# A hybrid decoder step: its first normalized input made one feature chunk at a time, with GpSimd scaling the sample tokens there

## The chip, the cores and the metric

The kernel runs on one core of one Trainium2 chip. A core has TensorE (PE, matrix products into PSUM), VectorE (DVE), ScalarE (ACT), GpSimd (POOL) and SyncE (SP, here used only to issue DMAs). The engines run their own instruction streams in order and meet by semaphores. The metric is the device time of one execution in microseconds, lower is better.

## The reference, cut to what matters

The model is a decoder trunk with two layers (`DEPTH = 2`), width 1024, run on 256 prompt tokens and 64 sample tokens (8 sequences of 8). Every layer is a SwiGLU of half weight, a token mixer and another such SwiGLU, and each of these sub-layers is normalized and modulated by vectors made from the conditioning `c` of its sequence:

```python
def modulate(h, shift, scale):
    return h * (1 + scale) + shift
...
    silu_c = jax.nn.silu(c)
...
        mod = (silu_c @ p['w_ada'][l] + p['b_ada'][l]).reshape(B, N_MOD, D)
        m = [mod[:, j][:, None, :] for j in range(N_MOD)]
        hh = modulate(rmsnorm(x, p['g_pre'][l, 0]), m[0], m[1])
```

There are nine modulation vectors of 1024 features for each layer. The first SwiGLU needs vector 0 (shift) and vector 1 (scale) of layer 0, which are a product of `silu(c)` (9 conditions: one prompt, eight samples) with 2048 columns of `w_ada`, 8 MB of weights. Later, the recurrent mixer of layer 1 needs `softplus(-rg_lambda)`, a function of 1024 parameters alone.

## The kernel before

Tokens are columns: 320 of them (256 prompt, 64 sample). Features are cut into `KC = 8` chunks of 128 partitions. Every product is made in three passes (`three_passes`, L1663 to L1667): a value is kept as a high and a low part, and high x high, low x high and high x low are summed in PSUM. So a weight tile that arrives in `w_raw` is split by ACT (`w_hi`, L1948) and DVE (`w_lo`, L2142), in two halves of 128x1024, and the normalized input by ACT (`xn_hi`, L2006) and DVE (`xn_lo`, L2218). A weight tile of the SwiGLU (`gu`) holds a gate block and an up block; its products are 2 blocks x 8 chunks x 3 passes = 48 matmuls of 128x320. The product of one tile with one chunk (6 matmuls) is called a unit below; unit (y, k) is tile y with chunk k.

The front is what comes before the first SwiGLU (`gate0`). SP issues the loads in a fixed order: `cT`, then pieces of `w_ada` (`a_raw`, 512 KB, six slots), `x`, small tables, further pieces, and the first half tiles of `gu` late. The plan is the table `ADA_PLAN`: a piece p holds contraction chunk p % 8 of vector p // 8. Each piece is four matmuls (`ada_pieces`, L1737) in four column groups of PE. A vector is complete only after its eight pieces. Then ACT copies it out (`ada_row`, L1962), PE turns it to feature rows with `sel4` (`ada_transpose`, L1756), and DVE adds the bias (`ada_bias`, L2153) and makes scale factors (`scale_factors`, L2162). Vector 0 takes pieces 0 to 7, vector 1 pieces 8 to 15. Small products of `ident` with `x` (`fill`, L1745) stand between pieces; their result is not used.

Beside that, ACT squares `x` (L1993), DVE sums the squares (L2417), PE sums over partitions (L1764), ACT and DVE make one over the root, PE spreads it (`spread`, L1772), and DVE scales `x` into `f` (`scale_x`, L2427). Once the vectors are there, ACT modulates the prompt columns of a chunk (`modulate`, L2001), DVE the sample columns of all chunks in a few instructions (L2228), ACT makes `xn_hi`, DVE `xn_lo`, and PE starts the units of the first two tiles (`two_tiles`, L1685), where tile 1 runs two chunks behind tile 0, so that units (1,5), (1,6) and (1,7) stand behind (0,7).

In the other stages GpSimd modulates the sample columns of chunks 2 to 7 (`samples`, L561 and L563). GpSimd also issues the `w_ada` pieces of the later stages (`ada_load`, L570).

After the first two tiles, `gate_up` runs 20 tiles more. Its start is a chain: when unit (0,7) is done, ACT splits the first half of tile 2 (L1948) and makes `sil` (L2026), DVE makes `w_lo` and `hbuf` (L2309), and PE may start tile 2 when `hbuf` is there. `gate1`, the second SwiGLU, starts in the same way behind `normed("gate1")` on DVE.

`softplus` is a row of small DVE instructions on 128x8, nearly all waiting for the one before. Its two first steps (L2433, L2435) and ACT's exponential (L2102) run in the front, the other 18 (L2441 to L2461, one of them eight times) inside the input projection of the attention stage (`dve_even`, at block 17).

## Time and profile before

| | |
|---|---|
| median of 3 runs | 1385.54 us |
| the runs | 1385.26 to 1385.80 us |
| span of the profiled execution | 1384.7 us |
| PE busy | 1340.4 us (97%) |
| DVE busy | 784.0 us (57%) |
| ACT busy | 621.2 us (45%) |
| GpSimd busy | 111.1 us (8%) |
| DMA, mean over the span | 188 GB/s |
| DMA, first of the 40 slices | 360 GB/s |

The profile is of one execution, whose span from first to last instruction is 1384.7 us; the device time of the runs is 0.8 us more than that. Records of PE overlap, since matmuls are pipelined: a matmul of 128x320 has a record of 0.31 us while the next one starts earlier. So the spacing of starts tells how fast PE works, not the length of a record. An fp32 matmul (the pieces, `fill`, `spread`) shows as two records.

### The profile page before, as it was taken

Reading aid. Unit: us, or ns where it says so; the run is one execution under the profiler, and the core shown is the slowest. Engines: PE = TensorE matmul, PEld = TensorE weight load, DVE = VectorE, ACT = ScalarE, POOL = GpSimd, SP = SyncE. Lnnn points to the kernel's source line nnn. Section 1 sums busy time; section 2 is a strip of 40 time slices with the busy share of each in tenths; the row PEclk is TensorE's granted clock in tenths of the full one; section 3 lists DMA queues with packets and bytes.
Section 4 is the critical chain, followed back from the end, with each engine's and each line's share of the span. In section 5 each row is a group of like instructions: output and inputs, shape, how many; then the busy total and the mean of one; then the engine's idle time right before and its main releaser. Section 6 shows DMA issues by size and latency. Waiting matters only on the chain.

```text
span 1384.7 us, 24435 instructions
## 1 busy us (share of the span) xinstructions
PE 1340.4 (97%) x9808; PEld 1260.8 (91%) x9808; DVE 784.0 (57%) x1410; ACT 621.2 (45%) x1059; POOL 111.1 (8%) x199
## 2 busy tenths in 40 slices
PE   6999999999999999999999999999999999999996
PEld 2899999989985789999999899999987989999996
DVE  2544444577787786444455744454577885444444
ACT  3543334453543555433434543344468745344432
POOL 0100000023011102000000200000020110000000
PEclk9999999999999999999999999999999999999998
DMA  9756556446459755564544546444455733444342
GB/s 360 267 210 210 191 180 224 163 157 221 131 192 354 286 193 204 173 217 142 178 156 165 195 148 236 147 164 164 166 219 180 280 116 127 152 146 148 125 146 81
DMA packets 82260, 260.02 MB, mean 188 GB/s; under 512 B 11634, under 2 KB 22962, under 8 KB 82034
## 3 DMA queue, kind: packets, MB, share of 16 engines
q1 hardware_dynamic: 65682, 199.49, 42.2%
q0 software_dynamic: 16480, 59.15, 11.7%
q8 instruction: 69, 1.13, 0.3%
q14 instruction: 29, 0.24, 0.1%
HBM read 254.38 MB, written 4.23 MB: 187 GB/s over the span
## 4 chain that ended last, share of the span: by engine, by line
PE 87%; DVE 5%; ACT 3%; DMA 2%; issue 2%; POOL 0%; SPq 0%; DVEq 0%; ACTq 0%
PE ps L1665 26%; PE ps L1666 26%; PE ps L1667 26%; PE ps L1737 3%; DVE w_lo L2142 1%; PE ps L1764 1%; DMA x<-in_x 1%; ACT w_hi L1948 1%; DVE f L2223 1%; PE ps L1772 1%; DVE x L2210 1%; DMA a_raw<-in_ada 1%; DMA lent_lo<-in_ada 0%; PE ps L768 0%; DVE f L2228 0%
## 5 line engine op out<-in xcount | busy, mean ns | idle before, releaser
L1665 PE MATMUL ps<-xn_hi,w_hi 128*128 128x320 f32 x1808 | 568.5, 314 | 12.2 <-DVE xn_lo L2218 7.0
L1667 PE MATMUL ps<-xn_hi,w_lo 128*128 128x320 f32 x1808 | 559.3, 309 | 0.0
L1666 PE MATMUL ps<-xn_lo,w_hi 128*128 128x320 f32 x1808 | 559.2, 309 | 0.0
L2142 DVE TENSOR_TENSOR w_lo<-w_raw,w_hi 128x1024 fp32r<-128x1024 f32 (+1 forms) x357 | 382.8, 1110 | 123.8 <-ACT w_hi L1948 123.5
L1948 ACT ACTIVATE w_hi<-w_raw 128x1024 fp32r<-128x1024 f32 x362 | 331.6, 961 | 87.5 <-PE ps L1667 76.8
L1665 PEld LDWEIGHTS ps<-xn_hi,w_hi 128*128 128x128 f32 x1808 | 339.9, 188 | 27.0 <-DVE xn_lo L2218 10.7
L1666 PEld LDWEIGHTS ps<-xn_lo,w_hi 128*128 128x128 f32 x1808 | 340.2, 188 | 1.0
L1667 PEld LDWEIGHTS ps<-xn_hi,w_lo 128*128 128x128 f32 x1808 | 339.9, 188 | 0.0
L1665 PE MATMUL ps<-mid_hi,w_hi 128*128 128x320 f32 x704 | 218.0, 310 | 0.4 <-DVE w_lo L2142 0.4
L1666 PE MATMUL ps<-mid_lo,w_hi 128*128 128x320 f32 x704 | 217.2, 309 | 0.0
L1667 PE MATMUL ps<-mid_hi,w_lo 128*128 128x320 f32 x704 | 217.2, 309 | 0.0
L2026 ACT ACTIVATE sil<-ps 128x320 f32<-128x320 f32 x88 | 38.4, 436 | 304.9 <-PE ps L1667 304.9
L2309 DVE TENSOR_TENSOR hbuf<-ps,sil 128x320 f32<-128x320 f32 x88 | 43.2, 491 | 228.1 <-ACT sil L2026 228.1
L1665 PEld LDWEIGHTS ps<-mid_hi,w_hi 128*128 128x128 f32 x704 | 132.2, 188 | 1.2 <-DVE w_lo L2142 0.6
L1666 PEld LDWEIGHTS ps<-mid_lo,w_hi 128*128 128x128 f32 x704 | 132.2, 188 | 0.0
L1667 PEld LDWEIGHTS ps<-mid_hi,w_lo 128*128 128x128 f32 x704 | 132.1, 188 | 0.0
L2314 DVE TENSOR_TENSOR mid_lo<-hbuf,mid_hi 128x320 fp32r<-128x320 f32 (+1 forms) x88 | 43.3, 492 | 49.7 <-ACT mid_hi L2030 49.7
L570 POOL DMA_DIRECT2D a_raw<-in_ada x76 | 40.3, 536 | 378.2 <-PE ps L1737 328.1
L2030 ACT ACTIVATE mid_hi<-hbuf 128x320 fp32r<-128x320 f32 (+1 forms) x88 | 41.5, 472 | 53.4 <-DVE hbuf L2309 53.4
L2039 ACT ACTIVATE sq<-ps 128x320 f32<-128x320 f32 x43 | 18.7, 435 | 102.2 <-PE ps L1667 102.2
L1737 PE MATMUL ps<-a_raw,c 128*32 128x256 f32 x736 | 50.9, 415 | 11.8 <-DMA a_raw<-in_ada 11.7
L2333 DVE TENSOR_TENSOR f<-ps,modT 128x64 f32<-128x64 f32 x40 | 8.9, 223 | 78.0 <-ACT f L2040 78.0
(297 smaller groups left out, 1029.8 us busy)
## 6 DMA issues: line engine op xcount, KB each, us to landing
w_raw<-in_gu SPq DMA_DIRECT2D x176, 512.0 KB, 4.6
a_raw<-in_ada POOLq DMA_DIRECT2D x76, 512.0 KB, 6.6
w_raw<-in_down SPq DMA_DIRECT2D x64, 512.0 KB, 3.6
w_raw<-in_pj SPq DMA_DIRECT2D x58, 512.0 KB, 4.8
w_raw<-in_down SPq DMA_DIRECT2D x64, 192.0 KB, 3.6
a_raw<-in_ada SPq DMA_DIRECT2D x16, 512.0 KB, 7.0
ex_xn<-in_ada POOLq DMA_DIRECT2D x16, 512.0 KB, 6.1
w_raw<-in_ada SPq DMA_DIRECT2D x16, 512.0 KB, 5.9
```

Source lines behind the costliest of these rows:

```text
L570: gp.dma_start(a_raw[:, r % A_SLOTS, :], row(t["ada"], p)).then_inc(a_landed[r % A_SLOTS], 16)
L1665: pe.matmul(out, hi, xhi, start=start, stop=False)
L1666: pe.matmul(out, hi, xlo, start=False, stop=False)
L1667: return pe.matmul(out, w_lo[s][:, w_at:w_at + P], xhi, start=False, stop=stop)
L1737: last = pe.matmul(ps[32 * g:32 * (g + 1), out, cols], c32[:, k, :], part[:, ADA_COLS * g:ADA_COLS * (g + 1)], start=(k == 0), stop=(k == ...
L1948: act.activation(w_hi[s][:, cols], w_raw[:, s, cols], ACT.Copy).then_inc(w_high, 1)
L2026: act.activation(sil[:, j, :], ps[:, 2 * j, 0:TOK], ACT.Silu).then_inc(sil_ready, 1)
L2030: act.activation(at(mid_hi, 2 * i + j), hbuf[:, j, :], ACT.Copy).then_inc(mid_high, 1)
L2039: act.activation(sqacc[:, :] if first else sq2[:, b, :], ps[:, bank, 0:TOK], ACT.Square).then_inc(sq_ready, 1)
L2142: dve.tensor_tensor(w_lo[s][:, cols], w_raw[:, s, cols], w_hi[s][:, cols].bitcast(F32), ALU.subtract).then_inc(w_split, 1)
L2309: dve.tensor_tensor(hbuf[:, j, :], ps[:, 2 * j + 1, 0:TOK], sil[:, j, :], ALU.mult)\
L2314: dve.tensor_tensor(at(mid_lo, 2 * i + j), hbuf[:, j, :], at(mid_hi, 2 * i + j).bitcast(F32), ALU.subtract).then_inc(mid_ready, 1)
```

## The change

The two vectors that the front needs are loaded in another cut: chunk c of the front holds the weights of the 128 shift and the 128 scale features of chunk c, for all eight contraction chunks (1 MB, `in_front`). So each load completes shift and scale of one feature chunk. Five of the eight have a buffer of their own, three use slots of `a_raw`. PE makes the eight matmuls of a chunk (`front_sums`), ACT copies the row, PE turns it (`front_turn`, two matmuls of 128x9, with a new part of `sel4` that also adds up the four column groups), DVE adds bias and makes the factor (`moved`), ACT modulates the prompt columns and GpSimd, new in this place, the sample columns. The units of the first two tiles stand between these steps on PE. Both tiles of `gu` are loaded between the chunks, and `x` in two halves ahead of all weights.

```diff
-ADA_PLAN = [("front", 0, KC), ("front", 1, 4), ("front", 2, 4)]
+ADA_PLAN = [("front", c, 2) for c in range(KC)]
...
+            sp_.dma_start(ident[:, :], t["ident"]).then_inc(const_in, 16)
+            sp_.dma_start(ones_d[:, :], t["ones_d"]).then_inc(const_in, 16)
+            for h in range(2):
+                half = slice(h * KC // 2, (h + 1) * KC // 2)
+                sp_.dma_start(x[:, half, :], t["x"][half].rearrange("k p n -> p k n")).then_inc(x_in[h], 16)
             sp_.dma_start(sel4[:, :], t["sel4"]).then_inc(sel_in, 16)
             sp_.dma_start(b_ada[:, :], t["b_ada"]).then_inc(bada_in, 16)
...
+            load_front(0)
+            load_w(t["gu"], 0, 0)
+            load_front(1)
+            load_front(2)
+            load_w(t["gu"], 1, 1)
+            for c in range(3, KC):
+                load_front(c)
...
+            def front_sums(c):
+
+                pe.wait_ge(fr_landed[c], 16)
+                part = front_slot(c)
+                for k in range(KC):
+                    g = k % 4
+                    last = pe.matmul(ps[32 * g:32 * (g + 1), B_ADA[c % 2], 0:ADA_COLS], c32[:, k, :],
+                                     part[:, ADA_COLS * k:ADA_COLS * (k + 1)], start=(k < 4), stop=(k >= 4))
...
+                fill(3)
+                stat_x("gate0")
+                front_sums(0)
+                pe.wait_ge(sel_in, 16)
+                spread(x_stat("gate0"), rx3, B_RY)
+                front_turn(0)
+                fill(4)
+                front_sums(1)
+                tile(0, 0)
+                front_turn(1)
+                front_sums(2)
+                tile(0, 1)
+                front_turn(2)
+                front_sums(3)
+                tile(0, 2)
+                front_turn(3)
+                tile(1, 0)
+                for c in range(4, KC):
+                    front_sums(c)
+                    tile(1, c - 3)
+                    front_turn(c)
+                    tile(0, c - 1)
+                tile(1, KC - 3)
+                tile(0, KC - 1)
+                tile(1, KC - 2)
+                tile(1, KC - 1)
```

On ACT the front is `copied(c)` (the row), the two halves of the split of a tile, and `chunk(c)` (wait for shift and scale, modulate the prompt columns, wait for GpSimd, make `xn_hi`), in one fixed order:

```diff
+                copied(0)
+                split_w(0, 0, only=(0,))
+                chunk(0)
+                split_w(0, 0, only=(1,))
+                copied(1)
+                chunk(1)
+                copied(2)
+                split_w(1, 1)
+                chunk(2)
+                for c in range(3, KC):
+                    copied(c)
+                    chunk(c)
```

On DVE, from chunk 3 on, the order is `moved(k)`, `scaled(k + 2)` (the old `scale_x` of one chunk) and `low(k)` (`xn_lo`). GpSimd's stream begins with the sample columns:

```diff
-            gp.wait_ge(w_landed[1][1], 16)
+            for c in range(KC):
+                gp.wait_ge(fr_mod, 2 * c + 2)
+                gp.wait_ge(xr_ready, c + 1)
+                fs = tokens(f[:, c, PTOK:TOK])
+                gp.tensor_tensor(fs, fs, per_sample(modT[:, scale_at(0, c), 1:NCOND]), ALU.mult).then_inc(fr_scaled, 1)
+                gp.wait_ge(fr_scaled, c + 1)
+                gp.tensor_tensor(fs, fs, per_sample(modT[:, shift_at(0, c), 1:NCOND]), ALU.add).then_inc(xmod_ready, 1)
+            gp.wait_ge(fr_landed[KC - 1], 16)
             ada_load(gp, pieces_of("gate0") + pieces_of("down0"))
...
-            dve_even(dve, steps, split_w, softplus, ada_bias)
+            dve_even(dve, steps, split_w, softplus_start, ada_bias)
             out_projection("even_out", EVEN_IN_TILES)
             invert(y_stat("even_out"), ry3)
             normed("gate1", "even_out")
+            softplus()
             gate_up(1)
```

`softplus` also moves. Its first two steps go to the place where the rest was, the exponential takes the place of an instruction on ACT that only had the table loaded, and the 18 DVE steps behind it now stand between `normed("gate1")` and `gate_up(1)`.

What stands in a row on PE at the front, before (`a_raw` is a piece, `x,ident` a `fill`, `sel` a turn, `ones_d` and `rx` the sum of squares and its spreading):

```order
L1737 MATMUL ps<-a_raw,c 32x256 x32
L1764 MATMUL ps<-ones_d,sqacc 107x64 x3
L1737 MATMUL ps<-a_raw,c 32x256 x16
L1756 MATMUL ps<-sel,ada_row 128x36 x2
L1772 MATMUL ps<-ident,rx 128x107 x3
L1745 MATMUL ps<-x,ident 128x128 x2
L1737 MATMUL ps<-a_raw,c 32x256 x4
...
L1756 MATMUL ps<-sel,ada_row 128x36 x2
L1745 MATMUL ps<-x,ident 128x320 x3
L1665 MATMUL ps<-xn_hi,w_hi 128x320
```

And in the changed kernel:

```order
L1751 MATMUL ps<-x,ident 128x320 x3
L1835 MATMUL ps<-ones_d,sqacc 107x64 x3
L1759 MATMUL ps<-front,c 32x256 x8
L1843 MATMUL ps<-ident,rx 128x107 x3
L1769 MATMUL ps<-sel,ada_row 128x9 x2
L1751 MATMUL ps<-x,ident 128x320 x4
L1759 MATMUL ps<-front,c 32x256 x8
L1677 MATMUL ps<-xn_hi,w_hi 128x320
L1678 MATMUL ps<-xn_lo,w_hi 128x320
L1679 MATMUL ps<-xn_hi,w_lo 128x320
```

The first product of a tile moves from behind all sixteen pieces to behind the second chunk of eight matmuls.

On DVE at the start of `gate1`, before, behind the last two `xn_lo` of the normalized input:

```order
L2218 TENSOR_TENSOR xn_lo<-f,xn_hi 128x320 x2
L2142 TENSOR_TENSOR w_lo<-w_raw,w_hi 128x1024
L2309 TENSOR_TENSOR hbuf<-ps,sil 128x320
L2142 TENSOR_TENSOR w_lo<-w_raw,w_hi 128x1024
L2314 TENSOR_TENSOR mid_lo<-hbuf,mid_hi 128x320
```

And in the changed kernel at the same place:

```order
L2305 TENSOR_TENSOR xn_lo<-f,xn_hi 128x320 x2
L2553 TENSOR_SCALAR sp<-sp 128x8
L2555 RECIPROCAL sp<-sp 128x8
L2557 TENSOR_TENSOR sp<-sp 128x8
L2559 TENSOR_TENSOR sp<-sp 128x8
L2561 TENSOR_SCALAR sp<-sp 128x8
L2564 SCALAR_TENSOR_TENSOR sp<-sp 128x8 x8
```

The steps of `softplus` now stand between the last `xn_lo` and the first `w_lo` and `hbuf` of `gate1`.

## Rows read from the trace of the kernel before

**Rows 1.** The page, busy time of each engine over the span.

```profile
PE 1340.4 (97%) x9808; PEld 1260.8 (91%) x9808; DVE 784.0 (57%) x1410; ACT 621.2 (45%) x1059; POOL 111.1 (8%) x199
```

**Rows 2.** Stretches: length, busy PE, PEld, DVE, ACT, POOL, clock, DMA share, GB/s.

```profile
4.00:36.00 32.00, 22.33 (x174) 9.91 (x174) 10.73 (x28) 10.50 (x21) 0.17 (x1) 1.00 1.01 386
41.60:53.05 11.45, 11.26 (x76) 11.00 (x76) 3.52 (x7) 6.43 (x12) 0.00 (x0) 1.00 0.77 287
```

**Rows 3.** Timeline of arrivals: start, length, what, idle before and its releaser.

```profile
15.68 2.98 ACT L1993 ACTIVATE sqx<-x 128x320 f32<-128x320 f32 x8 [12.24 <-DMA x<-in_x]
17.94 1.08 PE L1737 MATMUL ps<-a_raw,c 128*32 128x256 f32 x8 [4.87 <-DMA a_raw<-in_ada]
35.83 3.33 POOL L570 DMA_DIRECT2D a_raw<-in_ada  x6 [35.25 <-DMA w_raw<-in_gu]
```

**Rows 4.** Timeline of PE: pieces one by one and in fours, and three fills.

```profile
11.99 1.08 PE L1737 MATMUL ps<-a_raw,c 128*32 128x256 f32 x8 [0.20 <-DMA a_raw<-in_ada]
...
22.06 3.60 PE L1737 MATMUL ps<-a_raw,c 128*32 128x256 f32 x32
...
27.35 0.64 PE L1737 MATMUL ps<-a_raw,c 128*32 128x256 f32 x8
...
33.43 1.86 PE L1745 MATMUL ps<-x,ident 128*128 128x320 f32 x6
...
60.28 1.93 PE L1737 MATMUL ps<-a_raw,c 128*32 128x256 f32 x32
```

**Rows 5.** Timeline from the first to the third tile of gate0.

```profile
36.05 0.38 PE L1665 MATMUL ps<-xn_hi,w_hi 128*128 128x320 f32 x1 [0.75 <-issue]
...
50.08 0.31 PE L1665 MATMUL ps<-xn_hi,w_hi 128*128 128x320 f32 x1
...
50.27 1.06 ACT L1948 ACTIVATE w_hi<-w_raw 128x1024 fp32r<-128x1024 f32 x1 [4.48 <-PE ps L1667]
...
53.05 0.42 PE L1665 MATMUL ps<-xn_hi,w_hi 128*128 128x320 f32 x1 [0.17 <-DVE hbuf L2309]
```

**Rows 6.** Timeline at the end of the front: turn on PE, bias and factor on DVE.

```profile
32.99 0.61 PE L1756 MATMUL ps<-sel,ada_row 128*128 128x36 f32 x4 [0.59 <-ACT ada_row L1962]
...
33.63 0.23 DVE L2153 TENSOR_TENSOR modT<-ps,b_ada 128x72 f32<-128x72 f32 x1 [2.24 <-PE ps L1756]
33.90 0.23 DVE L2162 SCALAR_TENSOR_TENSOR modT<-modT,g_pre 128x72 f32<-128x72 f32 x1
```

**Rows 7.** Timeline of gate1's input: sample steps on DVE, a chunk on ACT and GpSimd.

```profile
516.23 0.49 DVE L2228 TENSOR_TENSOR f<-f,modT 128x64 f32<-128x64 f32 x2
...
524.23 0.60 ACT L2001 ACTIVATE f<-f,modT 128x256 f32<-128x256 f32 x1 [0.39 <-DVE f L2223]
...
524.28 0.48 POOL L561 TENSOR_TENSOR f<-f,modT 128x64 f32<-128x64 f32 x1 [0.99 <-DVE f L2223]
...
524.83 0.30 POOL L563 TENSOR_TENSOR f<-f,modT 128x64 f32<-128x64 f32 x1
...
525.22 0.47 ACT L2006 ACTIVATE xn_hi<-f 128x320 fp32r<-128x320 f32 x1 [0.39 <-POOL f L563]
...
530.81 0.37 ACT L1962 ACTIVATE ada_row<-ps 128x256 f32<-128x256 f32 x1
```

**Rows 8.** Timeline of softplus on DVE: first and last of 18 steps.

```profile
339.57 0.17 DVE L2441 TENSOR_SCALAR sp<-sp 128x8 f32<-128x8 f32 x1
...
342.80 0.16 DVE L2461 TENSOR_SCALAR spl8n<-sp 128x8 f32<-128x8 f32 x1
```

**Rows 9.** Timeline of DVE and PE at the start of gate1.

```profile
529.42 0.49 DVE L2218 TENSOR_TENSOR xn_lo<-f,xn_hi 128x320 fp32r<-128x320 f32 x1 [1.13 <-ACT xn_hi L2006]
...
532.38 1.23 DVE L2142 TENSOR_TENSOR w_lo<-w_raw,w_hi 128x1024 fp32r<-128x1024 f32 x1 [2.47 <-ACT w_hi L1948]
...
533.53 0.48 DVE L2309 TENSOR_TENSOR hbuf<-ps,sil 128x320 f32<-128x320 f32 x1
...
534.10 0.39 PE L1665 MATMUL ps<-xn_hi,w_hi 128*128 128x320 f32 x1
```

More of the change, by code:

```diff
@@ L133 @@
 A_ROWS = 6
+FRONT_OWN = 5
 def turns(stage, i):
@@ new lines, in front_turn, with front_stage, tile @@
+            def front_turn(c):
+                pe.wait_ge(fr_row, c + 1)
+                for h in range(2):
+                    col = (2 * c + h) * NCOND
+                    last = pe.matmul(ps[:, B_MOD, col:col + NCOND], ada_row[:, c % A_ROWS, h * P:(h + 1) * P],
+                                     sel4[:, 4 * NCOND:5 * NCOND], start=True, stop=True)
+                last.then_inc(fr_sel, 1)
+            def front_stage():
+                n = W_BASE["gate0"]
+                def tile(y_, k):
+                    if y_ == 0:
+                        pe.wait_ge(xn_ready, k + 1)
+                    for b in range(2):
+                        if k == 0:
+                            w_half(n + y_, b)
+                        last = three_passes(ps[:, 2 * y_ + b, 0:TOK], (n + y_) % 2, (b * KC + k) * P, xn_hi[:, k, :],
+                                            xn_lo[:, k, :], k == 0, k == KC - 1)
+                    if k == KC - 1:
+                        last.then_inc(w_used, 1)
+                pe.wait_ge(const_in, 16 * 2)
+                pe.wait_ge(x_in[0], 16)
+                fill(3)
[24 more added lines that the diff above has]
+                tile(1, KC - 1)
@@ L2098, in _ @@
             n_half[0] = 0
-            act.wait_ge(x_in, 16)
             squares_x("gate0")
-            act.wait_ge(sp_e, 1)
-            steps.did(act.activation(sp[1][:, :], sp[0][:, :], ACT.Exp, scale=-1.0))
             sqrt_table()
             root_front()
-            ada_copy(*turns("front", 1))
-            split_w(0, 0, only=(0,))
-            ada_copy(*turns("front", 2))
-            split_w(0, 0, only=(1,))
-            modulate("gate0")
+            front_stage()
             gate_up(0)
@@ L2424, in scale_x @@
                 dve.tensor_copy(mean_x[:, :], ps[0:TN, B_YSUM, 0:WIDE * NTC:WIDE])
+                steps.wait()
                 dve.wait_ge(r_ready, x_stat("gate0"))
[L2426 to L2427 removed]
+                scaled(0)
+                moved(0)
+                split_w(0, 0, only=(0,))
+                scaled(1)
+                low(0)
+                split_w(0, 0, only=(1,))
@@ L2429, in softplus_start @@
+                scaled(2)
+                moved(1)
+                scaled(3)
+                low(1)
+                scaled(4)
+                moved(2)
+                split_w(1, 1, only=(0,))
+                low(2)
+                split_w(1, 1, only=(1,))
+                for k in range(3, KC):
+                    moved(k)
+                    if k + 2 < KC:
+                        scaled(k + 2)
+                    low(k)
             def softplus_start():
                 z, w = sp[0], sp[2]
-                dve.wait_ge(lam_in, 16)
+                dve.wait_ge(late_in, 16 * 3)
```

184 lines of the change are left out of this document (89 added, 95 removed).

## Prediction, made before the changed kernel was run

> **What bounds the kernel now.** The page comes first: PE is busy 97% of the span [rows 1], so only its idle or half-used time can be won. Most of that lies at the front. The table of stretches shows the front from 4 to 36 us with 386 GB/s at a DMA share of 1.01 [rows 2]: the transfers are full, and PE starts the first real product at 36.05 [rows 5]. From 41.6 to 53.05 the same table has PE at its pace, 76 matmul records in 11.45 us, some 0.146 us for a matmul of 128x320 (0.875 us for a unit of six) [rows 2]. Tile 2 starts at 53.05 [rows 5]. From there on the kernel is the same work in the same order up to gate1, so I forecast one landmark, the start of tile 2, and add what else moves.
>
> The tail of this landmark matters. Unit (1,5), behind (0,7), starts at 50.08 and tile 2 at 53.05 [rows 5]: 2.97 us, of which 18 matmuls fill 2.63. ACT's split starts at 50.27, and PE is released by `hbuf`.
>
> **The change: arrivals.** `x` (1.31 MB) comes 3.69 us behind the sixth piece (15.68 after 11.99) [rows 3, 4], and small tables and a piece 2.26 us after it (17.94) [rows 3]; a piece alone is about 1.3. From the eighth piece (19.2, 1.28 behind the seventh) to all of tile 1's weights (35.83 at the latest) [rows 3] 12 half-MB loads take 16.4 us, 1.37 each. The changed kernel orders the same bytes as tables, `x`, chunk 0, tile 0, chunks 1 and 2, tile 1, chunks 3 to 7. With the stream starting near 4.2: tables 4.5, `x` 8.2, tables 8.9 to 9.2, chunk 0 at 11.7, then 2.73 per MB: tile 0 14.4, chunk 1 17.2, chunk 2 19.9, tile 1 22.6, chunks 3 to 7 at 25.4, 28.1, 30.8, 33.6 and 36.3. The last chunk is thus later than the last piece was; the gain must come from products made before it.
>
> **PE's own work.** The same piece takes 1.08 us at 11.99 and 17.94, and 0.64 at 27.35 [rows 3, 4]; four pieces in a row take 3.60 at 22.06 and 1.93 at 60.28 [rows 4]. The granted clock reads 1.00 in all of the front [rows 2], so it doesn't tell the two apart, but the ratio is that of 1.2 and 2.4 GHz. PE had worked with pauses of 0.2 us and more until 20 us, and without from 20.8; the faster pace came within the group at 22.06. A chunk's eight matmuls are two pieces: 0.97 us at the fast pace, 1.8 at the slow one. A fill is 0.62 (1.86 for three) [rows 4] or 1.07. Fills, sum of squares and chunk 0 keep PE busy from about 10 to 15, so I take the fast pace from about 16. Chunk 0's matmuls then end at 13.8, spreading and turn (some 0.6 to 0.9 each, as the turn in [rows 6]) near 15.4, four fills at 18, chunk 1's matmuls at 19.1. Unit (0,0) waits for the second half of tile 0's `w_lo`, some 19.8: done 20.4.
>
> **The loop of one chunk.** From the start of a turn to its bias step is 0.64 (32.99 to 33.63), two DVE steps of about 0.2 follow (the wide ones took 0.23 each [rows 6]), then ACT 0.60 beside GpSimd, `xn_hi` starts 0.99 after them (524.23 to 525.22) and takes 0.47 [rows 7], `xn_lo` 0.49: about 3.05 from turn to unit. ACT copies the next chunk's row (0.37 [rows 7]) only behind `xn_hi`, so one turn can follow another at about 3.0. PE's own row for a chunk is a turn (0.61 alone [rows 6], taken as 0.4 where other matmuls follow), matmuls 1.0 and two units 1.75: 3.15. The two are close; PE is the longer. Turns 1 and 2, each with the loop exposed and the split of tile 1 on ACT and DVE between, come at 20.4 and 24.1; unit (0,2) waits for the split and ends near 27.9. From turn 3 at 27.9 four periods of 3.15 give turn 7 at 40.5, where chunk 7 (landed 36.3) has long been there. Then 3.05 to unit (0,7), 0.875 for it: 44.45. Behind it stand only two units, but the chain to `hbuf` is as before, 2.97: tile 2 at 47.4, and 47.6 with a little for the handoffs. Against 53.05 that is **5.45 us won**. Some 1.2 us of PE idleness before tile 2 (the missing third unit) is in this number.
>
> **Softplus.** It leaves a place where PE waited for nothing of it, so nothing is won there. Its 18 steps last 3.39 us (339.57 to 342.96) [rows 8]. At gate1 the last `xn_lo` ends at 529.91, and DVE then stands idle 2.47 us until `w_lo` at 532.38; `hbuf` ends at 534.01 and PE starts the next tile at 534.10 [rows 9]. With 3.39 us put into a gap of 2.47, `w_lo` starts at 533.3, `hbuf` ends at 534.95, and PE starts at 535.0: **0.9 us lost**. Queued behind the softplus steps on DVE are both halves of `w_lo`, `hbuf` and `mid_lo`; PE waits for `hbuf`. Bounds: nothing, if a turn on PE hid it (that turn is already hidden in the 534.10), and 1.5.
>
> **GpSimd.** Its two steps take 0.48 and 0.30 and end 0.9 after their start, beside ACT's 0.60, where DVE makes two such steps in 0.49 [rows 7]. So GpSimd, not ACT, sets `xn_hi`, by about 0.3 per chunk. That counts once in the landmark, on the last chunk, and is in the 0.99. In the Trainium skill, "GPSIMD Engine Reference", section "Engine selection" advises VectorE for elementwise work, with GpSimd about twice as slow for two inputs. This trace is a little milder (0.78 against 0.49 for the pair); by the rule the pair would take 0.98, and the time 0.2 us more. GpSimd's own loads for gate0 now stand behind these steps and start near 43 in place of 35.83 [rows 3]; the first is wanted at tile 3, 7 us after tile 2, that is at 54.6: hidden, by about 4 us after a flight of some 7. The second table load of ACT and the other two softplus steps leave the front off its path: nothing.
>
> **Sum.** The profiled execution has 1384.7 us, 0.8 less than its device time, and both terms are differences: 1385.5 - 5.45 + 0.9 = **1381.0 us**.
>
> **Rivals.**
> - The loop is longer than the row of PE. If from turn to turn it is 3.6 rather than 3.15 (each of its six handoffs 0.1 slower, or the copy later), four periods cost 1.8 more: 1382.8. For it: the two lie within 0.15. Against: rows 7 hold handoffs already.
> - The fast pace comes late, with or after chunk 1. Four fills take 4.3, chunk 1's matmuls 1.8, the first unit 1.75: about 2.3 later, and the loop after it carries this to the end, since chunk 7 leaves only slack on the DMA side: 1383.3.
> - The slow pace stays or returns (slower). PE stands idle in the changed front for 0.5 to 1.4 us at a time between chunks 1 and 3, where at present it paused 0.2 us between pieces and stayed slow from 5 to 20 us. At the slow pace the row of a chunk is 1.8 + 3.5 + 0.45 = 5.75, 2.6 more each. With the 2.3 above, it turns into a loss beyond 0.2% from two chunks on; three give 1391.1. Against: with a row of 5.75 PE would have no pauses left, which is what ended the slow pace at 22. The Trainium skill, "TensorE: Matmul & The Clock Gate", Part 1, has the array at half rate by default and after idleness, and at full rate after sustained work; the trace agrees (3.60 and 1.93), and by it this rival hangs on the pauses.
> - PE waits only for data. If handoffs cost nothing and the loop is short, the floor is chunk 7 at 36.3: matmuls, unit, turn by 38.6, then 3.05, 0.875 and 2.97: tile 2 at 45.4, and 1378.8.
> - Softplus costs nothing: 1380.1, inside the forecast's own range.
>
> **Chances.** Forecast with softplus either way, 0.57 (1379.5 to 1382.7); long loop 0.13, half of it beyond 1382.8; late pace 0.12; floor 0.09; slow pace 0.09. A measurement of this kernel tells about 0.2% (2.8 us) from no change, so faster means below 1382.8: 0.57 + 0.06 + 0.09, and a little of the late pace: 0.74. Slower means above 1388.3: 0.09. The rest, 0.17, is the same. The range leaves out the slow pace and the end of the floor: 1377.8 to 1385.0.
>
> **What would show it.** Right: tile 2's first matmul near 47.6; chunks landing every 2.7 us and the last near 36; turns 3 to 7 about 3.15 apart; `hbuf` at gate1 behind 3.4 us of small DVE steps and PE idle 0.9 us there. Wrong: matmuls of the first units spaced nearer 0.29 us than 0.146 (pace), waits of the turn for `ada_row` (loop) or of the chunk matmuls for DMA (arrivals), or GpSimd steps well over 0.5 us beside DVE's.

## The result, and the profile after

| | before | changed |
|---|---|---|
| median of 12 runs each, interleaved | 1385.67 us | 1390.30 us |
| the runs | 1383.83 to 1389.29 | 1382.74 to 1395.21 |
| ratio | | 1.0028, 95% interval 1.0015 to 1.0041 |
| the same pair again on another occasion (35 and 12 runs) | 1387.03 us | 1387.67 us; ratio 1.0005, interval 0.9991 to 1.0019 |
| span of the profiled execution | 1384.7 us | 1393.3 us |
| start of tile 2 | 53.05 us | 55.23 us |

The forecast was 1381.0 us (1377.8 to 1385.0). The change brought no gain: by the medians 4.6 us are lost in the first comparison and 0.6 in the second, which alone can't be told from zero. By the means of their runs the two together give a ratio of 1.0018 (1.0008 to 1.0027 by resampling the runs), some 2.4 us slower. The landmark, forecast at 47.6, came at 55.23, that is 2.2 us later than before where 5.45 earlier was expected. The profiled execution is the longest of the changed kernel's twelve (1395.21 us), so its span overstates what the change costs. One execution of the kernel before (1637.41 us at a mean granted clock of 0.754) and one of a version below (2184.73 us at 0.558) were in a slow state and are left out of all ratios, intervals and means.

The page of the changed kernel, busy time of each engine, answers to [rows 1]. PE is busy 6 us longer, part of it by the half clock told below:

```profile
PE 1346.5 (97%) x9820; PEld 1267.8 (91%) x9820; DVE 785.3 (56%) x1420; ACT 622.5 (45%) x1063; POOL 117.3 (8%) x215
```

The timeline of PE in the front of the changed kernel (start, length, line, tiles, how many, and in brackets the idle time ahead of it with its releaser) answers to [rows 4, 5, 6]. L1751 is `fill`, L1835 the sum of squares, L1759 a chunk's products, L1843 `spread`, L1769 a turn, L1677 the first matmul of a product group. Fp32 matmuls show as two records.

```profile
8.04 3.54 PE L1751 MATMUL ps<-x,ident 128*128 128x320 f32 x6 [8.04 <-DMA x<-in_x]
12.97 1.34 PE L1835 MATMUL ps<-ones_d,sqacc 128*107 128x64 f32 x6 [1.40 <-DVEq L2492]
14.24 1.94 PE L1759 MATMUL ps<-front,c 128*32 128x256 f32 x16
16.11 1.34 PE L1843 MATMUL ps<-ident,rx 107*128 107x107 f32 x6
17.29 0.53 PE L1769 MATMUL ps<-sel,ada_row 128*128 128x9 f32 x4
17.67 2.40 PE L1751 MATMUL ps<-x,ident 128*128 128x320 f32 x8
...
22.80 0.41 PE L1677 MATMUL ps<-xn_hi,w_hi 128*128 128x320 f32 x1 [0.98 <-DVE w_lo L2229]
...
23.35 0.51 PE L1769 MATMUL ps<-sel,ada_row 128*128 128x9 f32 x4
...
26.14 0.42 PE L1677 MATMUL ps<-xn_hi,w_hi 128*128 128x320 f32 x1 [1.29 <-DVE xn_lo L2511]
...
30.84 0.63 PE L1677 MATMUL ps<-xn_hi,w_hi 128*128 128x320 f32 x1 [2.20 <-DVE xn_lo L2511]
...
38.23 0.51 PE L1769 MATMUL ps<-sel,ada_row 128*128 128x9 f32 x4
...
48.41 0.51 PE L1769 MATMUL ps<-sel,ada_row 128*128 128x9 f32 x4
...
51.21 0.42 PE L1677 MATMUL ps<-xn_hi,w_hi 128*128 128x320 f32 x1 [0.44 <-DVE xn_lo L2511]
...
55.23 0.42 PE L1677 MATMUL ps<-xn_hi,w_hi 128*128 128x320 f32 x1 [1.12 <-DVE hbuf L2381]
```

Read it by the idle times in brackets. PE never waits for a chunk's load, so the new order of the loads did its part. From chunk 0's products to unit (0,7) every pause is for `xn_lo` or `w_lo` of DVE. Ahead of unit (0,2) PE stands 2.20 us. The matmul behind that pause has a record of 0.63 us where the others of its kind have 0.42, and the stretches of the same kernel (columns as in [rows 2]: length, busy PE, PEld, DVE, ACT, POOL, granted clock, DMA share, GB/s) say why:

```profile
24.00:28.00 4.00, 2.71 (x34) 1.95 (x30) 1.87 (x8) 3.23 (x5) 0.59 (x2) 1.00 1.03 426
28.00:32.00 4.00, 1.80 (x16) 1.29 (x9) 2.79 (x4) 1.34 (x3) 1.50 (x2) 0.84 1.00 420
32.00:36.00 4.00, 4.00 (x22) 3.26 (x24) 1.25 (x4) 1.07 (x2) 0.59 (x2) 0.50 1.01 390
36.00:40.00 4.00, 4.00 (x36) 2.87 (x32) 0.76 (x3) 1.01 (x3) 0.59 (x2) 0.81 0.77 306
```

From 30.7 on, for 6.8 us, the granted clock is 0.50. That is 1.2 in place of 2.4 GHz. The drop begins at the end of the pause of 2.20 us, and in the stretch ahead of that pause, from 24 to 28 us, PE had been busy for 2.71 of 4 us. The stretch from 32 to 36 has 22 matmul records where full pace gives some 40.

What holds `xn_lo` up stands in the timelines of GpSimd, DVE and ACT, in this order, which answer to [rows 7]. L2623 and L2625 are GpSimd's two steps of a chunk:

```profile
18.40 1.21 POOL L2623 TENSOR_TENSOR f<-f,modT 128x64 f32<-128x64 f32 x1 [17.80 <-DVE modT L2505]
...
24.34 0.29 POOL L2623 TENSOR_TENSOR f<-f,modT 128x64 f32<-128x64 f32 x1 [4.36 <-DVE modT L2505]
...
28.11 1.21 POOL L2623 TENSOR_TENSOR f<-f,modT 128x64 f32<-128x64 f32 x1 [3.11 <-DVE modT L2505]
```

```profile
18.23 1.21 DVE L2229 TENSOR_TENSOR w_lo<-w_raw,w_hi 128x1024 fp32r<-128x1024 f32 x1
...
24.17 0.48 DVE L2497 TENSOR_TENSOR f<-x,ps 128x320 f32<-128x320 f32 x1
...
27.95 1.22 DVE L2229 TENSOR_TENSOR w_lo<-w_raw,w_hi 128x1024 fp32r<-128x1024 f32 x1
```

```profile
20.07 0.47 ACT L2069 ACTIVATE xn_hi<-f 128x320 fp32r<-128x320 f32 x1 [1.12 <-POOL f L2625]
```

GpSimd's first step of a chunk takes 0.29 to 0.30 us in six chunks and 1.21 in two. In those two DVE had begun its 128x1024 step of `w_lo`, with both inputs in SBUF, 0.17 and 0.16 us earlier, and GpSimd's step ends 0.17 and 0.15 us behind it. A DVE step beside it isn't enough: in chunk 1 `scale_x`, with one of its two inputs in PSUM, ran from 24.17 to 24.65, and GpSimd's step of 24.34 took 0.29. ACT waits 1.12 us for it in chunk 0, and again in chunk 2 where it waits 0.20 otherwise.

At the start of the second gate stage, DVE and PE in the changed kernel, to be read against [rows 8, 9]:

```profile
537.03 0.17 DVE L2553 TENSOR_SCALAR sp<-sp 128x8 f32<-128x8 f32 x1
...
540.33 0.17 DVE L2573 TENSOR_SCALAR spl8n<-sp 128x8 f32<-128x8 f32 x1
...
540.40 1.22 DVE L2229 TENSOR_TENSOR w_lo<-w_raw,w_hi 128x1024 fp32r<-128x1024 f32 x1
...
541.54 0.48 DVE L2381 TENSOR_TENSOR hbuf<-ps,sil 128x320 f32<-128x320 f32 x1
...
542.08 0.41 PE L1677 MATMUL ps<-xn_hi,w_hi 128*128 128x320 f32 x1 [0.61 <-DVE hbuf L2381]
```

The softplus steps last 3.47 us, `w_lo` stands right behind them, and PE now waits 0.61 us for `hbuf`. From the first to the second sigmoid step of this stage it is 2.97 us, and it was 2.17 before: 0.8 lost.

### The profile page after: what moved, and what is told of

It is laid out like the page before. It is cut to its first block, busy times and chain, and to the rows that moved or that the text cites. A ratio compares the mean times of both kernels' runs of the same rounds, so it can differ in the third digit from the quotient of the medians.

```text
span 1393.3 us, 24499 instructions
## 1 busy us (share of the span) xinstructions
PE 1346.5 (97%) x9820; PEld 1267.8 (91%) x9820; DVE 785.3 (56%) x1420; ACT 622.5 (45%) x1063; POOL 117.3 (8%) x215
## 4 chain that ended last, share of the span: by engine, by line
PE 86%; DVE 6%; ACT 3%; DMA 2%; issue 2%; POOL 1%; SPq 0%; DVEq 0%; ACTq 0%; POOLq 0%
PE ps L1677 26%; PE ps L1679 26%; PE ps L1678 26%; PE ps L1743 3%; DMA lent_lo<-in_ada 2%; DVE w_lo L2229 1%; PE ps L1835 1%; PE ps L1843 1%; DVE f L2310 1%; ACT w_hi L2013 1%; DVE x L2297 1%; PE ps L1759 0%; DVE xn_lo L2305 0%; DMA x<-in_x 0%; DVE f L2293 0%
## 5 line engine op out<-in xcount | busy, mean ns | idle before, releaser
L1677 PE MATMUL ps<-xn_hi,w_hi 128*128 128x320 f32 x1808 | 571.0, 316 | 16.3 <-DVE xn_lo L2305 6.6
L1677 PEld LDWEIGHTS ps<-xn_hi,w_hi 128*128 128x128 f32 x1808 | 341.1, 189 | 34.0 <-issue 12.3
L1677 PE MATMUL ps<-mid_hi,w_hi 128*128 128x320 f32 x704 | 218.0, 310 | 0.3 <-DVE w_lo L2229 0.3
L1677 PEld LDWEIGHTS ps<-mid_hi,w_hi 128*128 128x128 f32 x704 | 132.1, 188 | 1.2 <-DVE w_lo L2229 0.6
L2064 ACT ACTIVATE f<-f,modT 128x256 f32<-128x256 f32 x48 | 28.7, 598 | 35.3 <-DVE f L2310 22.5
```

The lines of the kernel that those rows point to most:

```text
L1677: pe.matmul(out, hi, xhi, start=start, stop=False)
L2064: steps.did(act.activation(f[:, k, 0:PTOK], f[:, k, 0:PTOK], ACT.Identity, scale=modT[:, scale_at(sub, k), 0:1], bias=modT[:, shift_at(sub ...
```

## Experiments

All timings are against the kernel before, interleaved. The first four comparisons share one set of 35 executions of it, the next four another, so within a group they are not independent. "Trace" is that of one profiled execution (the expectations call it a look). The table at the end of this section has all traces side by side.

**The changed kernel again.** No edit.

> The changed kernel as it is, once more. Theory A (the clock): where PE waits for 2 us in the front, the granted clock falls in some executions and not in others, so this trace may show tile 2 earlier than 55.2 us with the granted clock at 1.00, or the same with 0.50 in a stretch; the runs should again lie several us apart, and the longer ones have the lower mean clock. Theory B (arithmetic of the front: the loop is 3.4 us and starts 3 us late): tile 2 starts at 52 us or later even with the clock at 1.00. Theory C (something behind the front is lost every time): the waits for the lent pieces in the attention stage are again 2 us and more, against 0.4 before.

Measured: 1387.67 us, ratio 1.0005 (0.9991 to 1.0019); tile 2 at 55.22, with the same drop of the clock at 30.8. The front came out as in the first trace. The whole does not repeat as well: single executions of one kernel lie up to 12 us apart, and over the 12 runs of the first comparison their time goes with their mean granted clock (correlation -0.87).

**Sample tokens on DVE.** GpSimd's two steps move behind `moved(c)` on DVE.

```diff
                 def moved(c):
...
+                    dve.wait_ge(xr_ready, c + 1)
+                    steps.did(dve.tensor_tensor(fs, fs, per_sample(modT[:, scale_at(0, c), 1:NCOND]), ALU.mult))
+                    steps.wait()
+                    dve.tensor_tensor(fs, fs, per_sample(modT[:, shift_at(0, c), 1:NCOND]), ALU.add).then_inc(xmod_ready, 1)
```

> The sample columns of the front are scaled and shifted by VectorE, right behind the factors of the chunk, and GpSimd does nothing there. If GpSimd's first step was held up by VectorE's split of a weight tile (1.21 us in two of eight chunks, 0.29 in the others), xn_hi of chunks 0 and 2 comes about 0.9 us earlier, PE's wait before unit (0,2) falls from 2.2 to about 1.6 us (the split then stands before xn_lo on VectorE), and the clock falls less often: 1 us from the front itself and up to 3 more from the clock. If GpSimd is not to blame, the wait stays at 2.2 us and the time where it was, near 1390.

Measured: 1385.74 us, ratio 0.9998 (0.9982 to 1.0013); tile 2 at 50.50. In this trace `x` had landed at 6.95 us in place of 8.04 and PE was at its fast pace from 12 us on, so early that it caught up with the loads:

```profile
25.53 1.93 PE L1759 MATMUL ps<-front,c 128*32 128x256 f32 x16 [1.84 <-DMA front<-in_front]
```

The chunk's sixteen records take 1.93 us here, not 1.07: the clock had dropped at 24.7, in this new pause. One wait went and the next in line, chunk 3's load, took its place.

**Fills in the pauses.** `fill(2)` ahead of `tile(0, 1)` and `fill(3)` ahead of `tile(0, 2)`.

```diff
                 front_sums(2)
+                fill(2)
                 tile(0, 1)
...
                 front_sums(3)
+                fill(3)
                 tile(0, 2)
```

> Two idle products before unit (0,1) and three before unit (0,2), where PE waited 1.3 and 2.2 us. Theory A: the granted clock stays 1.00 through the front, nothing on the path is later by more than 0.1 us, tile 2 starts near 52, and the runs get 2 to 3 us shorter and closer together. Theory B and C: tile 2 is where it is without the fills in an execution whose clock did not fall, and the median does not move by more than 1 us.

Measured: 1385.74 us, ratio 0.9996 (0.9981 to 1.0010); tile 2 at 51.74, 3.5 us earlier than without the fills. Of that, 0.47 us was there at turn 0 already (16.82 in place of 17.29), ahead of the edit, since `x` landed 0.40 earlier. They compute nothing that is used. The stretches of this kernel beside those of the changed one above:

```profile
28.00:32.00 4.00, 3.61 (x22) 2.69 (x19) 2.43 (x4) 0.94 (x3) 1.15 (x2) 1.00 1.00 420
32.00:36.00 4.00, 4.00 (x38) 3.19 (x36) 1.86 (x7) 1.77 (x4) 0.86 (x3) 1.00 1.01 389
```

The clock stays at 1.00, and 38 matmul records stand where 22 stood. From turn 0 to tile 2 it is 34.9 us in place of 37.9. All four traces with the 2.20 us pause have a drop within 0.9 us of its end. None of the nine traces with these fills has one there (two have one earlier in the front, at 14.0 and 25.8); so the drop was a result of PE's pauses, and cost some 3 us.

**Softplus inside the second gate stage,** behind the last tile pair's `ada_bias`.

```diff
             normed("gate1", "even_out")
-            softplus()
             gate_up(1)
...
+                        if (ff, i, j) == (1, 5, 1):
+                            softplus()
```

> The 18 small steps on VectorE stand behind the twelfth tile of gate1 rather than ahead of its first. The gap of PE before the third tile of gate1 goes from about 0.6 us back to nothing, and the distance from the start of that stage's first sil to its second is again 2.16 us as in the kernel before, against 2.97: 0.8 us less, in every execution. In the median this may hide among runs that lie 10 us apart. The rival, that these steps cost nothing, leaves the distance at 2.97.

Measured: 1387.06 us, ratio 1.0000 (0.9984 to 1.0015); 2.17 us between the two sigmoid steps, as before the change. DVE and PE there:

```profile
535.21 1.23 DVE L2229 TENSOR_TENSOR w_lo<-w_raw,w_hi 128x1024 fp32r<-128x1024 f32 x1 [2.47 <-ACT w_hi L2013]
...
536.35 0.49 DVE L2381 TENSOR_TENSOR hbuf<-ps,sil 128x320 f32<-128x320 f32 x1
...
536.92 0.39 PE L1677 MATMUL ps<-xn_hi,w_hi 128*128 128x320 f32 x1
```

The gap of 2.47 us is that of [rows 9], and PE's wait is gone. The 0.8 us belong to the softplus.

**DVE's big steps kept apart from GpSimd's.** The low halves of the first two tiles' weights stand behind `low(0)` and `low(2)`.

```diff
                 moved(0)
-                split_w(0, 0, only=(0,))
                 scaled(1)
                 low(0)
-                split_w(0, 0, only=(1,))
+                split_w(0, 0)
...
                 moved(2)
-                split_w(1, 1, only=(0,))
                 low(2)
-                split_w(1, 1, only=(1,))
+                split_w(1, 1)
```

> The changed kernel with VectorE's low halves of the first two weight tiles put behind the low parts of chunks 0 and 2, so that no 128x1024 step of VectorE runs beside GpSimd's two steps of those chunks. Theory (the two engines hold each other up): GpSimd's first step of chunks 0 and 2 falls from 1.21 us to 0.3, and the two VectorE steps stay at 1.21 or fall by a little; the second product unit still waits for its low weights, so that little of the 0.9 us a time is won in chunk 0, and 0.9 us in chunk 2. If TensorE's wait before unit (0,2) falls below some 1.3 us, the clock stays at 1.00 there and tile 2 starts near 51.5 us; if not, near 54. Rival (the first GpSimd step after a pause is slow by itself): it stays at 1.2 us in chunk 0 whatever VectorE does. Time of the whole: 0 to 4 us below that of the changed kernel, within its spread of plus and minus 4.

Measured: 1385.23 us, ratio 0.9995 (0.9981 to 1.0009); tile 2 at 53.13, the clock at 1.00 in all of the front. The group of GpSimd's first steps over the front (line, shapes, count, busy, mean ns of one, idle):

```profile
L2621 POOL TENSOR_TENSOR f<-f,modT 128x64 f32<-128x64 f32 x8 | 2.4, 298 | 42.0 <-DVE modT L2505 42.0
```

All eight take 0.3 us, the first among them, so the rival falls. The pause ahead of unit (0,2) is 1.30 us in place of 2.20. In this trace PE was slow until some 22 us, so its tile 2 is later than the order of work alone would have it; the third trace of the changed kernel, slow until 22 too, has the 2.20 us pause and the drop.

**The three together** (fills, big steps apart, softplus inside; GpSimd keeps the samples).

> The changed kernel with three edits: 2 and 3 fill products ahead of units (0,1) and (0,2), the low halves of the weights behind the low parts as in the run before, and the softplus back inside the second gate stage. GpSimd keeps the sample tokens. Theory (terms add up): no drop of the granted clock in the first 60 us, tile 2 at 50 to 51 us, and 2.17 us between the two sigmoid steps at the second gate stage; the whole 3 us (front 2 to 3 us against the kernel before, softplus nothing lost) below the kernel before, ratio 0.998. Rival (what is won in front is given back in the attention stage, in every execution): ratio 1.000 with tile 2 at 50 us all the same.

Measured: 1385.49 us, ratio 0.9987 (0.9970 to 1.0004); tile 2 at 51.56. The clock did drop, at 14.0 for 6.8 us, ahead of everything that the edits touch. Neither the theory's place of tile 2 nor the rival's came out; the ratio lies between them and tells neither.

**Fills, samples on DVE, softplus inside.**

> As the run before, but VectorE scales and shifts the sample tokens too, and the low halves of the weights stand where the changed kernel has them. Theory (GpSimd's hand-over, not the order of the loads, costs the front its time): no drop of the granted clock in front, tile 2 at 47.5 to 49 us, the whole 4 to 5 us below the kernel before, ratio 0.9970. Rival (VectorE becomes the bound of the loop, since two steps of 0.3 us more stand in each period): a period of 3.5 us or more from turn 3 on, tile 2 at 51 or later, ratio 0.999 to 1.000.

Measured: 1386.07 us, ratio 0.9991 (0.9979 to 1.0002); tile 2 at 49.60, turns 3.39 us apart as in the changed kernel, so DVE's further steps are hidden and the rival falls. From turn 0 to turn 1 it is 5.23 us, and 6.06 with the fills alone; from turn 2 to turn 3 it is 4.03 and 4.70. Both traces were fast from 16 us and had no drop there, so 0.83 and 0.67 us is what GpSimd's part costs the front in chunks 0 and 2. Tile 2 is 3.45 us earlier than before in this trace, while the means of the runs differ by 1.1 us.

**The same with chunk 0's products ahead of the statistic,** and ACT's copy of chunk 0 ahead of the root.

```diff
-                stat_x("gate0")
                 front_sums(0)
+                stat_x("gate0")
                 pe.wait_ge(sel_in, 16)
```

> As the run before, with chunk 0's products ahead of the sum of squares' on TensorE and the copy of chunk 0's row ahead of the root on ScalarE: the chunk lands near 11.5 us and its products need not stand behind the statistic, which comes at 13. Theory: statistic from 13.5 instead of 12.97, spread at 15.5 instead of 16.1, all of the front 0.6 us earlier: tile 2 at 47 to 48.4 us, ratio 0.9965. Rival (the pause before the statistic, now broken by the products, was not on the path): tile 2 within 0.2 us of the run before.

Measured: 1386.83 us, ratio 1.0003 (0.9987 to 1.0018); tile 2 at 52.04, later rather than earlier. `spread` came at 15.51 (15.23 without the edit): the statistic, now at 13.51, with the root and the reciprocal behind it, is the longer way. In this trace the four fills took 4.62 us from 17.63, while the granted clock read 1.00. That the edit itself made PE slow does not follow, as the next runs show.

**The kernel before, twice more.**

> The kernel before, unchanged, for a second look. It asks whether what differs behind the front belongs to the change. Theory A (the granted clock and the lent pieces of the attention stage vary from execution to execution in both kernels): tile 2 again at 53.05 us to within 0.1, but the stretch from the last sigmoid step of the first gate stage to that of the second (327.0 us in the first look) differs by 1 to 3 us, with drops of the granted clock at other places or lengths, and TensorE waits between 0.4 and 2.5 us for the lent pieces. Theory B (the attention stage of the changed kernels is slower by its own doing): 327.0 again to within 0.5, one drop of 3.4 us, and 0.4 us of waits for the lent pieces.

> The kernel before once more, a third look, as for the run ahead of it: by theory A another set of drops and waits, by theory B the same 327.0 us. Also the drop of 6.8 us near 1125 us, which costs 3.0 us: by theory A it comes in some looks and not in others.

Measured: spans 1387.6 and 1383.5 us, tile 2 at 53.31 and 53.04, the stretch between the two gate stages 328.9 and 328.1 us after 326.9 in the first trace. Two stretches of the first trace and the same two of the third:

```profile
470.00:490.00 20.00, 17.67 (x160) 17.09 (x157) 13.38 (x34) 13.01 (x25) 5.32 (x10) 0.91 0.99 379
1120.00:1140.00 20.00, 17.51 (x144) 13.99 (x143) 14.03 (x38) 8.05 (x16) 3.98 (x5) 0.83 0.23 80
```

```profile
470.00:490.00 20.00, 17.67 (x157) 17.10 (x156) 12.37 (x33) 12.55 (x24) 5.31 (x10) 0.83 0.99 379
1120.00:1140.00 20.00, 16.98 (x161) 13.73 (x161) 17.18 (x44) 9.54 (x20) 4.70 (x7) 1.00 0.27 90
```

The first trace has 3.4 us of half clock near 476 and 6.8 near 1125, the third 6.8 and none. So the drops move from execution to execution in an unchanged kernel (theory A). The one near 1125 alone costs some 3 us: from the third gate stage's first sigmoid step to the fourth's it is 370.1 to 370.6 us in traces with it and 366.8 to 367.3 in traces without. Both later traces of before also have a drop of 3.4 us near 38 us, and tile 2 is not moved by more than 0.3: there PE had time to spare.

**Fills, samples on DVE, softplus inside, for a second time.**

> The version with fills, the sample tokens on VectorE and the softplus inside the second gate stage, for a second time with as many rounds. Its front: tile 2 at 49.6 us to within 0.3, where no drop of the clock falls into it. The whole: with tile 2 3.45 us earlier and no softplus lost, 3.4 us below the kernel before at the same mean granted clock (ratio 0.9975); the rival, that the attention stage takes back part of what comes earlier because its pieces land no earlier, gives 1 us (0.9992, as in its first run).

Measured: 1386.29 us, ratio 0.9988 (0.9973 to 1.0002). By means, both comparisons of this kernel together give 0.9990, with 0.9982 to 0.9998 by resampling their runs. But tile 2 was at 51.99, without any drop of the granted clock: the theory's 49.6 fell, and with the same program. The first records of PE show where it comes from. This kernel's first trace, then its second:

```profile
12.10 1.34 PE L1837 MATMUL ps<-ones_d,sqacc 128*107 128x64 f32 x6 [1.39 <-DVEq L2496]
...
16.51 0.53 PE L1769 MATMUL ps<-sel,ada_row 128*128 128x9 f32 x4
16.89 2.40 PE L1751 MATMUL ps<-x,ident 128*128 128x320 f32 x8
```

```profile
12.30 1.34 PE L1837 MATMUL ps<-ones_d,sqacc 128*107 128x64 f32 x6 [1.39 <-DVEq L2496]
...
16.85 0.90 PE L1769 MATMUL ps<-sel,ada_row 128*128 128x9 f32 x4
17.59 4.62 PE L1751 MATMUL ps<-x,ident 128*128 128x320 f32 x8
```

**The changed kernel, a third trace.**

> The changed kernel once more, a third look. Theory (front as told): tile 2 at 55.2 us to within 0.1, with the clock drop of 6.8 us near 30.8; GpSimd's first step 1.21 us in chunks 0 and 2. Rival (the drop falls there by chance): tile 2 near 53, without a drop ahead of 60 us.

Measured: tile 2 at 56.10, again with the drop, now at 32.5. PE was slow until 22 us here too. That costs more than the 0.9 us by which tile 2 is later than in the first trace, since `x` landed 0.77 us earlier (7.27).

**A fourth fill in the pause ahead of the statistic,** in the version with fills, samples on DVE and softplus inside; three traces, and a third trace without it.

```diff
-                fill(3)
+                fill(4)
                 stat_x("gate0")
```

> The version with fills, sample tokens on VectorE and softplus inside the second gate stage, with a fourth fill (1.14 us at the slow pace) in TensorE's pause of 1.4 us ahead of the statistic. Theory (the pause sets when the fast pace comes): fast from some 12 us on, so that statistic, chunk 0's products and spread take 2 us less together (chunk 0's 16 products 1.0 instead of 1.9 us), and tile 2 at 47.5 to 48 us, ratio 0.9980. Rival (the place is chance, whatever stands there): fast from 12, 16.5 or 22 us as before, tile 2 between 47.5 and 52, ratio 0.999.

> The same kernel, a second look. Theory: again fast from 12 us, tile 2 within 0.3 of the run before. Rival: another of the three places.

> The same kernel, a third look, with the same expectations as the second.

> The version without the fourth fill, a third look: fast from 16.5 or 22 us (tile 2 at 49.6 or 52.0), as in the two looks on record; from 12 us (tile 2 near 47.5) would speak for chance.

Measured: fast from 12 us on in all three traces, tile 2 at 49.47, 51.10 and 48.07; without it, slow until 22 once more, tile 2 at 52.67. PE in the first trace with four fills:

```profile
7.48 4.61 PE L1751 MATMUL ps<-x,ident 128*128 128x320 f32 x8 [7.48 <-DMA x<-in_x]
12.41 0.80 PE L1837 MATMUL ps<-ones_d,sqacc 128*107 128x64 f32 x6 [0.32 <-DVEq L2496]
13.14 1.07 PE L1759 MATMUL ps<-front,c 128*32 128x256 f32 x16
...
15.28 2.40 PE L1751 MATMUL ps<-x,ident 128*128 128x320 f32 x8
```

The pause is 0.32 us in place of 1.4 and the chunk takes 1.07 in place of 1.94. With the pause 2 of 11 traces were fast from 12 us, 5 from 16 and 4 from 22 (the version with chunk 0 first, whose order there is another, is not counted); without it 3 of 3 from 12. That points to the pause as what lets chance in, on three traces. The gain is eaten in part: chunk 3's load is then late (1.4, 1.7 and 0.2 us of wait), and one trace has a drop at 25.8 behind that wait. The timed runs give 1386.39 us, ratio 0.9996 (0.9982 to 1.0011); the best single traced execution took 1380.66 us.

**All traces.** "`x` at" is the start of PE's first record, which `x` releases: it lies between 6.95 and 8.04 us and shifts what stands behind it, so places of tile 2 compare only to about 1 us. The fast pace is read from the spacing of PE's starts; a drop is a stretch with the granted clock at 0.50, given by start and length, near 1125 by its length. "Between" is from the last sigmoid step of the first gate stage to the first of the second; the lent pieces are PE's waits for them in it, in total.

| trace | `x` at | fast from | tile 2 | drop in front | between | lent | near 1125 | span |
|---|---|---|---|---|---|---|---|---|
| before | - | - | 53.05 | none | 326.9 | 0.4 | 6.8 | 1384.7 |
| before, second | - | - | 53.31 | 38.5, 3.4 | 328.9 | 1.4 | 6.8 | 1387.6 |
| before, third | - | - | 53.04 | 38.0, 3.4 | 328.1 | 0.5 | none | 1383.5 |
| changed | 8.04 | 16 | 55.23 | 30.7, 6.8 | 331.9 | 2.5 | 6.8 | 1393.3 |
| changed, second | 7.77 | 16 | 55.22 | 30.8, 6.8 | 329.1 | 1.5 | 6.8 | 1389.8 |
| changed, third | 7.27 | 22 | 56.10 | 32.5, 6.8 | 330.0 | 1.9 | none | 1388.7 |
| samples on DVE | 6.95 | 12 | 50.50 | 24.7, 6.8 | 328.6 | 1.8 | none | 1381.5 |
| fills | 7.64 | 16 | 51.74 | none | 328.6 | 1.4 | none | 1382.8 |
| softplus inside | 7.11 | 16 | 54.06 | 29.4, 6.8 | 328.8 | 0.9 | none | 1385.0 |
| steps apart | 7.89 | 22 | 53.13 | none | 327.5 | 0.9 | none | 1383.1 |
| three together | 7.68 | 12 | 51.56 | 14.0, 6.8 | 329.2 | 1.7 | none | 1383.3 |
| fills, DVE, softplus | 7.16 | 16 | 49.60 | none | 330.3 | 1.4 | none | 1382.0 |
| the same, chunk 0 first | 7.00 | 22 | 52.04 | none | 330.4 | 1.5 | none | 1384.8 |
| fills, DVE, softplus, second | 7.37 | 22 | 51.99 | none | 328.0 | 1.2 | 6.8 | 1384.8 |
| the same, third | 7.92 | 22 | 52.67 | none | 333.8 | 2.0 | 6.8 | 1392.3 |
| with a fourth fill | 7.48 | 12 | 49.47 | none | 333.3 | 1.6 | none | 1384.9 |
| the same, second | 7.16 | 12 | 51.10 | 25.8, 3.4 | 328.7 | 1.7 | 6.8 | 1384.6 |
| the same, third | 7.05 | 12 | 48.07 | none | 329.1 | 2.3 | none | 1379.0 |

## Why the prediction was wrong

**The frame held.** One landmark and one further term: the first gate stage carries the shift of tile 2 to its end unchanged (154.1 to 154.2 us from its first to its last sigmoid step in every trace). Arrivals held too: no wait of PE for a chunk in the changed kernel. The step that failed is the course of PE and the loop of one chunk, from 8 us to turn 7: the working put turn 0 at 15.4 without a term for the chain of the statistic, took GpSimd's step at its length in [rows 7] with nothing for the DVE step beside it, and left what a pause costs by the clock out of the sum, to a rival with 0.09. Forecast and measured, by the changed kernel's rows:

| | forecast | measured | late by |
|---|---|---|---|
| turn 0 | 15.4 | 17.29 | 1.9 |
| turn 1 | 20.4 | 23.35 | 2.95 |
| turn 2 | 24.1 | 27.13 | 3.0 |
| turn 3 | 27.9 | 32.60 | 4.7 |
| turn 7 | 40.5 | 48.41 | 7.9 |
| tile 2 | 47.6 | 55.23 | 7.6 |

- **Start, 1.9 us.** The working had chunk 0's products end at 13.8. They stand behind the sum of squares in PE's order, which came at 12.97 since DVE's sum ends only then, and they end at 16.2. The working took the two side by side. Nor is it the order alone: with chunk 0's products first, `spread` came at 15.51, where it stood at 15.23 without that edit, so the row of DVE's sum, the statistic, the root and `spread` wanted a term of its own.
- **GpSimd beside DVE, 1.0 us in chunk 0 and some 0.85 in chunk 2.** Forecast: 0.3 a chunk, in the 0.99 already. Both sizes are measured less forecast; between two traces, the samples on DVE gave back 0.83 and 0.67. The forecast took its GpSimd price from [rows 7], "beside ACT". DVE's row at the same moment of that trace, of the kernel before, shows the hold already:

```profile
524.11 0.48 DVE L2218 TENSOR_TENSOR xn_lo<-f,xn_hi 128x320 fp32r<-128x320 f32 x1
```

GpSimd's 0.48 us step of 524.28 in [rows 7] began 0.17 behind this one, which has two SBUF inputs too, and ended 0.17 behind its end; the step after it took 0.30. So the 0.48 held a wait of 0.2 us behind a DVE step of 0.48, and behind one of 1.21 the wait is 0.9. The order of DVE's work puts `split_w(..., only=(0,))` right behind `moved(0)` and `moved(2)`, at the moment at which GpSimd is released. The run with the steps apart shows the cause: 298 ns each, eight times. The Trainium skill has this in "SBUF — State Buffer", section "SBUF: two separate sides": whichever of a DVE step with two SBUF inputs and a GpSimd step that reads SBUF starts first keeps the shared port to its end, and the other is fully blocked. The trace agrees where DVE came first: GpSimd's step ends 0.15 to 0.17 us behind DVE's whether that lasts 0.48 or 1.21. That DVE is held when GpSimd comes first, no run here shows. The rule weighed in the prediction, that GpSimd takes about twice as long, did not decide anything here: alone GpSimd takes 0.29 us a step, and the pair less than the 0.78 of [rows 7].
- **The clock, 3.1 us.** The six matmuls of unit (0,2) at the half pace (0.88 us more), and turn 3 to turn 4 5.63 us in place of 3.39 (2.24 more). Between traces with and without the fills it is 3.0. The rival "slow pace returns" had the mechanism and the condition, PE's pauses between chunks 1 and 3, and got 0.09. Of the slow rows that it counted one came, turn 3 to turn 4 at 5.63 us where it had 5.75, and not two or three, since the drop ended after 6.8 us. It was set against 0.5 to 1.4 us of pause; the GpSimd term made it 2.20. Two terms that were weighed apart work together: the run with the steps apart lost both, in its one trace, the run with fills the second alone.
- **The loop, 0.96 us.** Four periods of 3.39 for 3.15. PE is the bound, as said, since the period is the same with the samples on DVE; but every change of tile costs a first matmul of 0.23 to 0.25 us in place of 0.146, and the products of the next chunk start 0.24 us behind the last matmul's start.
- From turn 7 on 0.25 us were won back. The terms add up to 7.6. Two small slips of the working change nothing: from 19.2 to 35.83 it is 16.6 us, not 16.4, and the floor's terms give 45.5, not 45.4.
- **Softplus** was right: 0.9 forecast, 0.8 measured, by the gap that was named. So was the statement that GpSimd's own loads, at 50.35 (forecast 43), are hidden.

**From the landmark to the whole.** The two terms give 2.2 + 0.8 = 3.0 us slower than before. The two comparisons gave 4.6 and 0.6 by their medians, and 2.4 together by their means. What makes them differ is not the change's alone: the stretch between the gate stages takes 326.9 to 328.9 us in three traces of before and 329.1 to 331.9 in three of the changed kernel, and the drop near 1125 comes in two of three traces of either.

**What stays open.** The longest single wait for a lent piece is 0.4 to 0.6 us in the three traces of before and 0.6 to 2.0 in the fifteen of all changed versions, and a drop of the clock between 415 and 437 us was seen in five of the fifteen and in none of the three. Those five have the longest stretches between the gate stages, 330.3 to 333.8 us; the other ten have 327.5 to 330.0. Issues of loads and products are the same up to there, only shifted. That the front's change makes this stage some 1 us dearer is possible and not shown, and three traces of before are few. The version with fills, samples on DVE and softplus inside has tile 2 at 51.4 in the mean of its three traces, 1.7 us won, and its runs show 1.4. That the two are close proves little: the same three traces take 330.7 us between the gate stages in the mean, where before has 328.0. With the fourth fill the traces have tile 2 at 49.5, 3.6 us won, and the means of the runs differ by 0.5; there something is given back that these traces don't settle.

Of the versions tried, only the one with fills, samples on DVE and softplus inside is below the kernel before by its joint interval, by 0.1% (1.4 us), less than one measurement of this kernel can tell. It is also the only one of them that was timed twice, and one of eight tried, so an interval that ends at 0.9998 is weak evidence of a gain.

## What to carry to other kernels

Before work is put on GpSimd, look what two-input step of DVE starts just ahead of it, both there and in the rows that its price is taken from. A pause that a change makes on TensorE costs twice, by itself and by the clock behind it, so price the pauses together, and where one can't be removed, fill it and measure. Where a kernel's time moves by more than the effect from run to run, time a landmark in several profiled executions of both kernels rather than one.
